# Convolution of the second mixer: products of 26 taps on ACT, sums of 1024 columns on DVE

## The reference, cut to what matters

```python
u = a * jax.nn.sigmoid(b)                       # 256 tokens x 512 channels
y = lax.conv_general_dilated(                   # depthwise, causal, 31 taps
    u, conv_w[:, None, :], window_strides=(1,), padding=[(CONV_WIDTH - 1, 0)],
    dimension_numbers=("NWC", "WIO", "NWC"), feature_group_count=CONV_CH) + conv_b
mu = jnp.mean(yf, axis=-1, keepdims=True)       # then a layer norm over the 512 channels
var = jnp.mean(jnp.square(yf - mu), axis=-1, keepdims=True)
yn = (yf - mu) * lax.rsqrt(var + EPS) * ln_w + ln_b
return jax.nn.silu(yn)
```

## Time and profile before

| | us |
|---|---|
| median of 3 runs | 1020.2 |
| lowest and highest | 1017.89, 1024.25 |
| the profiled execution, device time | 1020.02 |
| its span in the trace | 1017.9 |
| PE busy in the span | 996.0 |
| DVE busy | 700.5 |
| ACT busy | 507.3 |

### The profile page before, as it was taken

One profiled execution on the slowest core, in us unless ns is written; L12 is line 12 of the kernel. 1 busy time (PEld: TensorE's weight loads), 2 busy tenths in 40 slices (PEclk: granted clock), 3 DMA queues, 4 the chain that ended last, 5 costly groups with the idle time before them and its releaser, 6 DMA issues.

```text
span 1017.9 us, 20023 instructions
## 1 busy us (share of the span) xinstructions
PE 996.0 (98%) x7393; PEld 938.5 (92%) x7393; DVE 700.5 (69%) x1284; ACT 507.3 (50%) x825; POOL 37.3 (4%) x52
## 2 busy tenths in 40 slices
PE   9999999999999999999999999899999999999996
PEld 8999999989988898999998899788899899998885
DVE  6766665545687769766676659978875488885553
ACT  6544454353466556654554465332664365444441
POOL 4500000010100000000000000000000000000000
PEclk9999999989999999999999999999999999999998
DMA  7545465436733345555565564313544255556451
GB/s 250 203 170 184 167 226 171 155 129 224 249 125 124 105 146 185 183 183 190 180 221 193 175 245 149 123 46 116 194 163 146 101 172 204 186 186 207 166 194 53
DMA packets 45980, 172.71 MB, mean 170 GB/s; under 512 B 5418, under 2 KB 6210, under 8 KB 45408
## 3 DMA queue, kind: packets, MB, share of 16 engines
q1 hardware_dynamic: 44352, 163.20, 46.5%
q0 software_dynamic: 1424, 8.65, 2.5%
q10 hardware_dynamic: 144, 0.03, 0.0%
HBM read 170.79 MB, written 3.77 MB: 171 GB/s over the span
## 4 chain that ended last, share of the span: by engine, by line
PE 82%; DVE 11%; ACT 3%; issue 2%; DMA 2%; SPq 0%; DVEq 0%; ACTq 0%
PE bank L391 19%; PE bank L392 18%; PE bank L393 18%; PE bank L395 11%; PE bank L396 6%; DVE cy L1402 3%; DVE wlo L369 3%; ACT whi L358 1%; PE bank L1200 1%; PE bank L406 1%; DMA raw<-in_w_mix 1%; DVE x L480 1%; DVE res L705 1%; PE bank L836 1%; PE bank L1585 1%
## 5 line engine op out<-in xcount | busy, mean ns | idle before, releaser
L391 PE MATMUL bank<-x,whi 128*128 128x256 f32 (+1 forms) x1464 | 419.4, 286 | 3.0 <-DVE x L480 1.9
L392 PE MATMUL bank<-x,whi 128*128 128x256 f32 (+1 forms) x1464 | 415.5, 284 | 0.0
L393 PE MATMUL bank<-x,wlo 128*128 128x256 f32 (+1 forms) x1464 | 413.5, 282 | 0.0
L369 DVE TENSOR_TENSOR wlo<-raw,whi 128x1024 fp32r<-128x1024 f32 (+1 forms) x285 | 359.6, 1265 | 20.7 <-ACT whi L358 20.7
L358 ACT ACTIVATE whi<-raw 128x1024 fp32r<-128x1024 f32 (+1 forms) x285 | 309.1, 1087 | 117.2 <-PE bank L393 73.3
L391 PEld LDWEIGHTS bank<-x,whi 128*128 128x128 f32 x1464 | 276.3, 189 | 11.6 <-issue 5.2
L392 PEld LDWEIGHTS bank<-x,whi 128*128 128x128 f32 x1464 | 276.2, 189 | 0.2
L393 PEld LDWEIGHTS bank<-x,wlo 128*128 128x128 f32 x1464 | 276.3, 189 | 0.0
L395 PE MATMUL bank<-hid,whi 128*128 128x512 f32 x432 | 151.3, 393 | 0.0
L396 PE MATMUL bank<-hid,wlo 128*128 128x256 f32 x432 | 120.5, 279 | 0.0
L395 PEld LDWEIGHTS bank<-hid,whi 128*128 128x128 f32 x432 | 80.9, 187 | 19.0
(11 more groups left out here) (276 smaller groups left out, 1213.6 us busy)
## 6 DMA issues: line engine op xcount, KB each, us to landing
raw<-in_w_f2in SPq DMA_DIRECT2D x44, 512.0 KB, 3.4
raw<-in_w_f1in SPq DMA_DIRECT2D x42, 512.0 KB, 3.4
raw<-in_w_mix SPq DMA_DIRECT2D x35, 512.0 KB, 3.5
raw<-in_w_up SPq DMA_DIRECT2D x32, 512.0 KB, 4.3
raw<-in_w_down SPq DMA_DIRECT2D x32, 512.0 KB, 4.3
raw<-in_w_f1out SPq DMA_DIRECT2D x16, 704.0 KB, 4.1
raw<-in_w_f2out SPq DMA_DIRECT2D x16, 704.0 KB, 4.1
raw<-in_w_mixb SPq DMA_DIRECT2D x20, 512.0 KB, 3.5
```

The costliest lines, as they stand in the source:

```text
L369: nc.vector.tensor_tensor(wlo[:, s, 0:tiles * P], raw[:, s, 0:tiles * P], whi[:, s, 0:tiles * P], ALU.subtract).then_inc(w_lo, 1)
L391: nc.tensor.matmul(out, whi[:, s, w], hi, start=first, stop=False)
L392: nc.tensor.matmul(out, whi[:, s, w], lo, start=False, stop=False)
L393: mm = nc.tensor.matmul(out, wlo[:, s, w], hi, start=False, stop=last)
```

## The change

The convolution is divided anew. Of each tile's 31 taps DVE keeps the first five (`OWN_TAPS`), 20 instructions of 128x256 as before, made in steps 4 to 10. The other 26 taps are made in two parts. For a tap, ACT multiplies each of the four tiles by its weights into one of four buffers `prod` (a Copy with a scale per partition, four instructions of 128x256), and DVE adds the four tiles to `cy` with one tensor_tensor of 128x1024. `ADDS` says how many such sums DVE makes at the end of each step: one in steps 11 to 15, two in 16, one in 17, two in 18, one in 19 and three in each of the steps 20 to 24. ACT makes the products for step `q+1` at the end of its step `q`, after `act_retention`. From the fifth product on ACT waits for the sum that frees the buffer, and a sum waits for its four products and for the sum before it. `prod` lies where `mem2` of the following stage lies. No DMA is added, removed or moved, and PE's list is the same except for the number that it waits for ahead of line 1241.

```diff
+OWN_TAPS = 5
+PRODS = 4
...
+        at = [mem2_at]
+        prod = place("prod", [P, PRODS, 4, NX], F32, at)
...
-        TAP0 = 4
-        TAPS_EARLY, TAPS_LATE = 5, 11
+        OWN = (0, 0, 0, 0, 3, 3, 2, 2, 4, 3, 3)
+        ADDS = (0,) * 11 + (1,) * 5 + (2, 1, 2, 1) + (3,) * 5
...
-        def taps_before(q):
-
-            n = (min(q, 20) - TAP0) * TAPS_EARLY + max(q - 20, 0) * TAPS_LATE
-            return min(n, 4 * TAPS)
+        def own_before(q):
+
+            return sum(OWN[:q])
+
+        def adds_before(q):
+
+            return sum(ADDS[:q])
+
+        CONV_STEPS = 4 * OWN_TAPS + TAPS - OWN_TAPS
...
-                    pe.wait_ge(conv_step, 4 * TAPS)
+                    pe.wait_ge(conv_step, CONV_STEPS)
...
                 if q >= RET0:
                     act_retention(act, q - RET0)
+                conv_products(act, adds_before(q + 1), adds_before(q + 2))
                 if q == LN0 + 2:
...
+        def conv_products(act, a, b):
+
+            for n in range(a, b):
+                j = OWN_TAPS + n
+                if n == 0:
+                    act.wait_ge(glu_done, 4)
+                    act.wait_ge(const_in, 48)
+                if n >= PRODS:
+                    act.wait_ge(conv_step, 4 * OWN_TAPS + n - PRODS + 1)
+                for t in range(4):
+                    nc.scalar.activation(prod[:, n % PRODS, t, :], glu[:, t, j:j + NX], ACT.Copy,
+                                         scale=convw[:, t * TAPS + j:t * TAPS + j + 1]).then_inc(prod_set, 1)
+
+        def conv_adds(dve, a, b):
+
+            for n in range(a, b):
+                dve.wait_ge(prod_set, 4 * n + 4)
+                dve.wait_ge(conv_step, 4 * OWN_TAPS + n)
+                nc.vector.tensor_tensor(cy[:, :, :], cy[:, :, :], prod[:, n % PRODS, :, :], ALU.add).then_inc(conv_step, 1)
+
         def conv_taps(dve, a, b):
 
-            for n in range(a, min(b, 4 * TAPS)):
-                t, j = n // (2 * TAPS) * 2 + n % 2, n % (2 * TAPS) // 2
+            for n in range(a, b):
+                t, j = n // (2 * OWN_TAPS) * 2 + n % 2, n % (2 * OWN_TAPS) // 2
...
-                if q >= TAP0:
-                    conv_taps(dve, taps_before(q), taps_before(q + 1))
+                conv_taps(dve, own_before(q), own_before(q + 1))
+                conv_adds(dve, adds_before(q), adds_before(q + 1))
```

More of the change, by code:

```diff
@@ L197, in build @@
         oz2 = place("oz2", [P, 8, 2, NX], F32R, at)
+        mem2_at = at[0]
         mem2 = place("mem2", [P, KT, 2, NX], F32R, at)
@@ L283, in build @@
         cs_act, cs_dve = sem("cs_act"), sem("cs_dve")
-        cb_sig, glu_done, conv_step = sem("cb_sig"), sem("glu_done"), sem("conv_step")
+        cb_sig, glu_done, conv_step, prod_set = sem("cb_sig"), sem("glu_done"), sem("conv_step"), sem("prod_set")
         rot_mm, rot_step, rg_done = sem("rot_mm"), sem("rot_step"), sem("rg_done")
@@ L1175, in build @@
         LN0 = 24
-        def taps_before(q):
-            n = (min(q, 20) - TAP0) * TAPS_EARLY + max(q - 20, 0) * TAPS_LATE
-            return min(n, 4 * TAPS)
-        assert taps_before(LN0) == 4 * TAPS
+        def own_before(q):
+            return sum(OWN[:q])
+        def adds_before(q):
+            return sum(ADDS[:q])
+        assert own_before(LN0) == 4 * OWN_TAPS and adds_before(LN0 + 1) == TAPS - OWN_TAPS
+        CONV_STEPS = 4 * OWN_TAPS + TAPS - OWN_TAPS
         RV = 12
```

## The result

The changed kernel takes 1030.46 us (median of 5 runs, 1027.03 to 1033.08), the kernel before 1020.2 (5 runs, 1017.89 to 1024.25): ratio 1.010, interval 1.0079 to 1.0122. The profiled execution is the one of 1030.46 us, with a span of 1028.3. The forecast was 1028.7 us in a range from 1019 to 1034.

A forecast was written before the change was run, and what follows sets the result against it. The prediction took PE, busy 98%, to set the time. Its terms, -2.1 early, +2.2 at step 16, +6.2 late and +2.5 for the clock, summed to 8.8 on 1020.0, given as 1028.7 us, range 1019 to 1034.

The forecast's parts named there:

- The early gain: Steps 4 to 13: DVE drops under PE's pace and PE's waits for it go, -2.1 us.
- The four waits: PE's waits for DVE in steps 8 to 13, rotary and bank read behind the taps: 0.7, 0.7, 0.4 and 0.3 us.
- The stop of step 16: Eight Copies on ACT delay the copy of value tile 2, so PE stops before the last value tile, +2.2 us.
- The late chain: Steps 19 to 24: ACT's 15 products and DVE's sums, chained together, delay line 1241 by +6.2 us.
- The clock: Steps 24 and 25: PE's idle gaps bring one fall to 1.2 GHz, between 0 and 3.4 us, taken at 2.5.
- The rival of two falls: The stop at step 16 also brings the clock down, another 3.4 us: 1032.1 us, chance 0.2.
- the waits of 2.5 and 3.3 us at the end: Steps 24 and 25: PE idle about 2.5 us ahead of line 1287 and 3.5 ahead of line 1241.
- The other side: Products vanish in ACT's idle time and only DVE counts, -2.1 early, +0.9 late: about 1018.8 us, chance 0.09.
- a lid on the gain: A faster convolution can give back only PE's waits, 2.1 us early and 1.4 us late, 0.35% of the time.

The follow-up runs named there:

- sums without products: Changed kernel without ACT's products; DVE makes the same 26 sums from the gated input, so the output is not the convolution: 1017.96 us, ratio 0.9972.
- half dose of fillers: Changed kernel with 4, 5 and 7 matmuls of unread results put in three PE waits of steps 16 and 25: 1023.47 us, ratio 1.0041.
- constant scale: Changed kernel with ACT's 104 product Copies taking a constant scale instead of the weight per partition: 1023.48 us, ratio 1.0045.
- mixed version: Changed kernel with 9 taps on DVE, 22 on ACT, sums placed anew, products ahead of the retention's part up to step 19: 1016.98 us, ratio 0.9976.
- products first: Changed kernel with ACT making its products ahead of the retention's part, not behind it, up to step 19: 1022.73 us, ratio 1.0033.
- mixed version with fillers: The mixed version plus 2 matmuls of unread results before the spread of step 25 and 1 before the channel sum: 1016.24 us, ratio 0.9962.

## Why the prediction was right, step by step

**The early gain** was forecast at 2.1 us and is 3.0 (turn at 57.81 us instead of 60.84, in all runs without the stop). The four waits are as the profile has them; but each also breaks PE's overlap of one matmul with the next, and the table of waits leaves that out. Up to the turn PE stood idle 3.05 us before and 0.84 us in the sums without products, which is 2.2 us; its busy time over the same matmuls fell from 57.79 to 56.97 us, which is the other 0.8. The step was read off the wait table and should have been read off the pace of the strips.

**The stop of step 16** was forecast at 2.2 us and is 2.1 (59.92 against 57.81). Its place in ACT's order was shown to be the cause by moving the pair away and by moving it ahead of the `yr` copy.

**The late chain** was forecast at +6.2 us and is +5.5 (keys to sum 34.21 against 28.73). Two prices were off, in opposite directions: a Copy has a pitch of 0.40 us, not 0.42 (12 in 4.88), which is 1.2 us over 60 of them; a sum in a run of three has 1.33 us, not 1.22 (three in 3.88). Of the 5.5 us, 2.9 go away with Copies that are a quarter cheaper, and 0.6 stay when there are no products at all. The 2.0 between are about 1.3 us in which DVE still waits for ACT's roots, roundings and products, and 0.7 us by which the sums are longer when they read `prod`. These come from the timelines of one execution each, and no run took ACT's order apart from its rate in steps 20 to 24.

**The clock** was forecast to fall once, late, for 2.5 us, and fell twice, for 3.1 and 3.0. This is the one step that failed: it is the sentence with which the prediction set the second fall aside, "Against: after it come full matmuls". Behind the gap, though, come first the small matmuls of turn, scores and values, and the strip only after them; the prediction had overlooked that, and the runs do not show whether it matters. The rival of two falls, with a chance of 0.2 and 1032.1 us, is what the profile shows. That the falls come from idle PE was shown by the half dose of fillers, which kept all the rest as it was. How many come, and how long they are, could not be read from one row: the gap of the earlier trace rows, 1.65 us in code that no edit here touches, has a fall behind it in six of the ten profiles of this study and none in four.

**The sum** of the prediction's terms, 8.8 on 1020.0, is 1028.8 and not 1028.7, which changes nothing. By measured terms it is -3.0 + 2.1 + 3.1 + 5.5 + 3.0 = +10.7 us of the stage, against +10.3 of the medians. The forecast's +8.8 came out of an early gain 0.9 too small, a late chain 0.7 too long and 3.6 of clock too little. The first two offset 1.6 us of the third, which is luck; the stop of step 16 and the waits of 2.5 and 3.3 us at the end, against 2.5 and 3.5 forecast, are not.

**The other side**, products that vanish in ACT's idle time, is refuted for this order and half true for another: put where ACT waits anyway, those of the steps up to 19 cost PE nothing (keys at 75.99 us with them and without). The rule of the Trainium skill (ScalarE: Activation LUTs, Rules for kernel authors) that multiplications belong on VectorE holds in its direction: for a tile of 128x256 a product alone took ACT 0.40 us, product and sum together took DVE 0.395, and the trade as made lost 1.0%. It doesn't hold to the end: with 22 of the 31 taps' products on ACT, at places where it waits, the kernel gained 0.2%.

## What to carry to other kernels

- Idle time of an in-order engine is not room for work; it lies between named instructions. Before work goes to it, list what stands behind the place on that engine and who waits for that. Here 41 us went to an engine that was half idle, 3.3 us of them in step 15 stopped PE, and the same instructions one place earlier did not.
- When the bound engine is TensorE, price a new wait at the wait plus the fall of the clock that may come behind it. In this stage a net 4.6 us of waits became 10.7 us by two falls of 3 us each.
- With a lid on the gain (3.5 us of waits) and none on the loss, move the least that removes the waits, not all that can be moved: 22 products instead of 26, nine instead of 15 of them late, and a better place for them together turned 1.0% of loss into 0.2% of gain. What each of the three is worth alone is shown only for the place.

## What the runs showed of the hardware

- A gap of 1.95 us, behind a full strip and ahead of the small matmuls of turn, scores and values, had 6.8 us at 0.50 behind it (from 656.56 us), while one of 1.21 us at the same place (constant scale) had none. In the profile of the mixed version 3.4 us at 0.50 stood behind waits of 0.9 and 0.8 us with 0.66 us of work between them. A single length of gap doesn't tell.
- The same gap does not tell either. In the first block PE stands idle for 1.65 us at 222 to 225 us, in code that no kernel here changes. Behind it the clock was 0.50 for 6.8 us in the profiles of the kernel before and of "products first", for 3.4 us in those of the changed kernel, the constant scale, the half dose of fillers and the mixed version with fillers, and not at all in the other four. "Products first" has one more such fall, at 262.6 us. Runs of one kernel lie up to 9 us apart, so single executions here are worth little, and medians of 5 to 22 runs were compared.
- A matmul of two f32 operands on 256 columns is two instructions and took 0.45 us in a row of them, not 0.22 (3.62 / 8, and 3.70 / 8 in a strip of keys).
- Three sums of 128x1024 in f32 on DVE, each waiting for the one before, took 3.88 us where they read ACT's products and 3.73 where they read the gated input: 1.33 and 1.26 us from one to the next, where one alone is 1.22 us long.
